# Two token blocks in another order at three stage boundaries of a hybrid decoder trunk

## The reference, cut to what matters

```
for l in range(2):
    h = rms_norm(x, attn_norm_g[l])
    x = x + hybrid_mixer(h, mem, w_in[l], ..., w_out[l])      # retention, forgetting attention, memory attention
    h = rms_norm(x, ffn_norm_g[l])
    if l % 2 == 0:
        x = x + (silu(h @ w_gate) * (h @ w_up)) @ w_down        # dense, D_FF = 2752
    else:
        x = x + moe_ffn(h, router_w, wg, wu, wd)                # top 2 of 8 experts
```

## Time and profile before

| what | value |
|---|---|
| median of three runs | 1327.45 us |
| fastest and slowest run | 1326.04 and 1327.48 us |
| span of the profiled execution | 1324.5 us |
| median less this span | 2.95 us |
| TensorE matmuls busy | 1248.4 us, 94% of the span |
| VectorE busy | 1011.2 us, 76% |
| ScalarE busy | 793.3 us, 60% |
| DMA, mean | 259 GB/s |
| mean granted clock of TensorE | 0.982 of full speed |

### The profile page before, as it was taken

How to read it: one execution, slowest core, us unless ns; L and a number is a source line. 1 busy time by engine, 2 the same in 40 slices (tenths; PEclk the granted TensorE clock), 3 DMA queues, 4 the chain that set the end, 5 groups by cost and what they waited for, 6 DMA issues and landing times.

```text
span 1324.5 us, 16360 instructions
## 1 busy us (share of the span) xinstructions
PE 1248.4 (94%) x6062; PEld 1037.6 (78%) x6062; DVE 1011.2 (76%) x988; ACT 793.3 (60%) x710; POOL 0.2 (0%) x4
## 2 busy tenths in 40 slices
PE   6998999999999869999999999989999998999996
PEld 4787788889787758887887887877887886887885
DVE  6878664444685778789788788887889886888885
ACT  4455354434446347677677677666667665667663
POOL 0000000000000000000000000000000000000000
PEclk9999899999999889999999999999999998999998
DMA  9842245546563138899899899898989998989970
GB/s 359 306 159 96 95 161 188 159 128 199 169 225 115 59 100 308 274 354 376 278 335 399 280 343 386 286 336 309 313 299 379 330 306 313 333 285 380 349 259 35
DMA packets 158798, 343.19 MB, mean 259 GB/s; under 512 B 5824, under 2 KB 47040, under 8 KB 158720
## 3 DMA queue, kind: packets, MB, share of 16 engines
q1 hardware_dynamic: 158720, 342.10, 74.3%
HBM read 341.02 MB, written 1.05 MB: 258 GB/s over the span
## 4 chain that ended last, share of the span: by engine, by line
PE 83%; DVE 10%; ACT 4%; issue 2%; DMA 0%; SPq 0%; DVEq 0%; ACTq 0%
PE ps L415 26%; PE ps L417 25%; PE ps L416 25%; DVE wlo L290 5%; ACT whi L283 3%; PE ps L644 1%; PE ps L465 1%; DVE scaled L1114 1%; PE ps L766 1%; PE ps L767 1%; PE ps L440 1%; PE ps L741 1%; PE ps L740 1%; DVE stlo L1124 1%; PE ps L514 0%
## 5 line engine op out<-in xcount | busy, mean ns | idle before, releaser
L290 DVE TENSOR_TENSOR wlo<-raw,whi 128x2048 fp32r<-128x2048 f32 (+3 forms) x356 | 741.3, 2100 | 237.6 <-ACT whi L283 237.2
L283 ACT ACTIVATE whi<-raw 128x2048 fp32r<-128x2048 f32 (+3 forms) x356 | 625.5, 1765 | 342.8 <-PE ps L417 341.3
L415 PE MATMUL ps<-whi,sthi 128*128 128x512 f32 (+4 forms) x1232 | 468.9, 381 | 21.7 <-DVE wlo L290 14.4
L417 PE MATMUL ps<-whi,stlo 128*128 128x512 f32 (+4 forms) x1232 | 457.9, 372 | 3.6 <-issue 3.6
L416 PE MATMUL ps<-wlo,sthi 128*128 128x512 f32 (+4 forms) x1232 | 458.5, 372 | 0.0
L415 PEld LDWEIGHTS ps<-whi,sthi 128*128 128x128 f32 x1232 | 233.8, 190 | 72.7 <-issue 22.7
L417 PEld LDWEIGHTS ps<-whi,stlo 128*128 128x128 f32 x1232 | 233.6, 190 | 39.0
L416 PEld LDWEIGHTS ps<-wlo,sthi 128*128 128x128 f32 x1232 | 234.3, 190 | 34.3
L415 PE MATMUL ps<-whi,hidhi 128*128 128x512 f32 (+1 forms) x440 | 176.6, 401 | 14.2 <-DVE wlo L290 11.4
L416 PE MATMUL ps<-wlo,hidhi 128*128 128x512 f32 (+1 forms) x440 | 172.3, 391 | 0.0
L417 PE MATMUL ps<-whi,hidlo 128*128 128x512 f32 (+1 forms) x440 | 172.2, 391 | 0.0
(11 more groups left out here) (191 smaller groups left out, 608.0 us busy)
## 6 DMA issues: line engine op xcount, KB each, us to landing
raw<-in_expert_w_down SPq DMA_DIRECT2D x80, 1024.0 KB, 6.8
raw<-in_expert_w_gate SPq DMA_DIRECT2D x64, 1024.0 KB, 7.3
raw<-in_expert_w_up SPq DMA_DIRECT2D x64, 1024.0 KB, 8.0
raw<-in_w_in SPq DMA_DIRECT2D x18, 1024.0 KB, 9.6
raw<-in_expert_w_gate SPq DMA_DIRECT2D x16, 768.0 KB, 6.1
raw<-in_expert_w_up SPq DMA_DIRECT2D x16, 768.0 KB, 5.1
raw<-in_dense_w_down SPq DMA_DIRECT2D x10, 1024.0 KB, 4.9
raw<-in_expert_w_gate SPq DMA_DIRECT2D x16, 640.0 KB, 4.2
```

The source lines that it names most:

```text
L283: eng.activation(whi[0:rows, n % SPLIT, 0:k * cols], raw[0:rows, n % RAW, 0:k * cols], ACT.Copy).then_inc(sem("hi_ready"), 1)
L290: eng.tensor_tensor(wlo[0:rows, n % SPLIT, 0:k * cols], raw[0:rows, n % RAW, 0:k * cols], whi[0:rows, n % SPLIT, 0:k * cols].bitcast(F32), ...
L415: pe.matmul(dst, xh, wh, start=start, stop=False)
L417: return pe.matmul(dst, xl, wh, start=False, stop=stop)
```

## The change

On TensorE, loads 2 and 3 of the out projection are taken as (2, block 0), (3, block 0), (2, block 1), (3, block 1). Between the last two stand the eight transposes of block 0's new `x`. The last two dense down loads go the same way. The units of a boundary are counted block by block: (0,0), (0,1), (1,0), (1,1). The first two loads of the dense gate and of the second input projection are taken block by block, and the eight transposes of block 1 stand behind the first twelve matmuls of block 0. Ahead of the router they stand right behind the out projection.

On ScalarE and VectorE, the split of the second load of the next stage moves into `next_turn`. VectorE has it behind block 0's units and ahead of the addition of block 1; ScalarE has it behind the squares of block 0 and ahead of block 0's units. ScalarE's squares of block 1 come ahead of block 1's units.

```diff
-                for q in range(4):
-                    m = n + 10 + q
-                    if q < 2:
-                        turn(f"out{l}", (2 * q, 2 * q + 1))
-                    pe.wait_ge(sem("lo_ready"), m + 1)
-                    for b in range(NB):
...
+                pe.wait_ge(sem("lo_ready"), n + 12 + 1)
+                mix_out(2, 0)
+                pe.wait_ge(sem("lo_ready"), n + 13 + 1)
+                mix_out(3, 0).then_inc(sem("block_summed"), 1)
+                mix_out(2, 1).then_inc(sem("weights_used"), 1)
+                turn(f"ffn{l}", (0, 1))
+                mix_out(3, 1).then_inc(sem("weights_used"), 1)
...
+            def first_gates(n):
+
+                for b in range(NB):
+                    for h in range(2):
+                        if b == 0:
+                            pe.wait_ge(sem("lo_ready"), n + h + 1)
+                        turned_in("ffn0", unit_of("ffn0", b, h))
+                        for k in range(4):
+                            last = product(ps[:, b, 0:CH[0]], P, stat(b, 4 * h + k), n + h, k, 4, CH[0], 0, CH[0],
+                                           start=(h == 0 and k == 0), stop=(h == 1 and k == 3))
+                        if b == NB - 1:
+                            last.then_inc(sem("weights_used"), 1)
+                        if b == 0 and h == 0:
+                            turn("ffn0", (2, 3))
...
+            pe.wait_ge(sem("lo_ready"), n + 1)
+            pe.wait_ge(sem("hid_lo"), NB * NCH - 1)
+            last_down(0, 0)
+            pe.wait_ge(sem("lo_ready"), n + 2)
+            last_down(1, 0).then_inc(sem("block_summed"), 1)
+            pe.wait_ge(sem("hid_lo"), NB * NCH)
+            last_down(0, 1).then_inc(sem("weights_used"), 1)
+            turn("att1", (0, 1))
+            last_down(1, 1).then_inc(sem("weights_used"), 1)
+
             mixer(1, IN1)
-            turn("ffn1")
+            turn("ffn1", (2, 3))
...
# ScalarE, next_turn
                 sum_squares(0)
-                used(act, n)
-                turn(name)
+                step(n - 1)
+                turn(name, (0, 1))
                 sum_squares(1).then_inc(sem("x_squared"), 1)
+                turn(name, (2, 3))
...
# VectorE, next_turn, inside the loop over the blocks
                     dve.tensor_tensor(xres[:, b, :], xres[:, b, :], flat(ps[:, at:at + 2, :]), ALU.add)\
                         .then_inc(sem("x_added"), 1)
-                turn(name)
-                if late is not None:
-                    step(late)
+                    turn(name, (2 * b, 2 * b + 1))
+                    if b == 0:
+                        step(n - 1)
...
# ScalarE and VectorE, ahead of next_turn
-                for q in range(3):
+                for q in range(2):
                     step(n + 10 + q)
```

More of the change, by code:

```diff
@@ L335, in build, with unit_of, place_of @@
         SCALED = {"att0": 0, "ffn0": 1, "att1": 2, "ffn1": 3}
-        UNITS = [(u % NB, u // NB) for u in range(2 * NB)]
+        def unit_of(name, b, half):
+            return 2 * b + half if name in X_ADDED else NB * half + b
+        def place_of(name, u):
+            return (u // 2, u % 2) if name in X_ADDED else (u % NB, u // NB)
         def turn_bank(name, u):
@@ L424, in turn @@
                 for u in units:
-                    b, half = UNITS[u]
+                    b, half = place_of(name, u)
                     src = xres if name in X_ADDED or name == "att0" else tok
@@ L621, in widths, with mix_out @@
-            def widths(kind, n, it, c, h, nb, par, bank, unit, fresh=None):
+                def mix_out(q, b):
+                    turned_in(f"out{l}", unit_of(f"out{l}", b, q // 2))
+                    for k in range(2):
+                        for half in range(2):
+                            last = product(ps[:, 2 * b + half, :], P, stat(b, 2 * q + k), n + 10 + q, k, 2, D,
+                                           half * W, (half + 1) * W, start=(q == 0 and k == 0), stop=(q == 3 and k == 1))
+                    return last
@@ new lines, in mixer @@
+                for q in range(2):
+                    turn(f"out{l}", (2 * q, 2 * q + 1))
+                    pe.wait_ge(sem("lo_ready"), n + 10 + q + 1)
+                    mix_out(q, 0)
+                    mix_out(q, 1).then_inc(sem("weights_used"), 1)
+                pe.wait_ge(sem("lo_ready"), n + 12 + 1)
[3 more added lines that the diff above has]
+                mix_out(2, 1).then_inc(sem("weights_used"), 1)
@@ L689, in _, with last_down @@
             n += 2
-            for h in range(2):
-                down(n + h, 0, NCH - 1, h, NB, NB * (NCH - 1), False, True)
-            turn("att1")
+            def last_down(h, b):
+                rows, nk, _ = ffn_shape("down", NCH - 1, h)
+                for k in range(nk):
+                    for half in range(2):
+                        last = product(ps[:, 4 + 2 * b + half, :], rows,
+                                       (hidhi[0:rows, b, 2 * h + k, :], hidlo[0:rows, b, 2 * h + k, :]), n + h, k, nk, D,
+                                       half * W, (half + 1) * W, start=False, stop=(h == 1 and k == nk - 1))
+                return last
+            pe.wait_ge(sem("lo_ready"), n + 1)
[7 more added lines that the diff above has]
+            last_down(1, 1).then_inc(sem("weights_used"), 1)
             mixer(1, IN1)
-            turn("ffn1")
+            turn("ffn1", (2, 3))
             pe.wait_ge(sem("router_lo"), 1)
@@ L1013, in _ @@
             n += 2
-            step(n)
             next_turn("att1", n + 1)
@@ L1209, in memory_turned, with next_turn @@
                 last.then_inc(sem("mk_T"), 1)
-            def next_turn(name, n, banks, late=None):
+            def next_turn(name, n, banks):
                 count = (n == DENSE0 - 1, n == IN1 - 1, n == MOE0 - 1).index(True)
```

31 lines of the change are left out of this document (19 added, 12 removed).

## The result

The changed kernel took 1330.78 us (median of seven runs, 1325.96 to 1332.5), the kernel before 1325.27 us beside it (seven runs, 1324.27 to 1327.48). The ratio is 1.0031, with a 95% interval of 1.0018 to 1.0045: 2.4 to 6.0 us slower. The span of its profiled execution is 1330.7 us against 1324.5.

The account below looks back on a forecast made before the run. TensorE, busy 94% of the span, was taken as the bound. Boundary shifts of -0.8, +0.5 and +3.95 us sum to +3.65 on 1327.45, giving 1331.1 us; own range 1329.6 to 1332.8, 8-in-10 range 1327.3 to 1332.8.

Parts of the forecast that it names:

- First boundary, -0.8: Out projection of layer 0 to dense gate: 0.8 us shorter, with bounds of -1.5 and 0.
- Second boundary, +0.5: Last two dense down loads to second input projection: 0.5 us longer by TensorE's waits, bounds -0.5 and +1.2.
- Third boundary, +1.45 by the waits: Out projection of layer 1 to router: 1.45 us longer by later units and logits, bounds +1.0 and +2.0.
- Third boundary, +2.5 by the clock: Router matmuls at 1.2 GHz after an emptier stretch: 2.5 us longer, at most 2.9, 0 if the clock stays.
- Rival 1: Third boundary: the clock holds through the emptier stretch, sum +1.15 us, 1328.6 us; chance 0.28.
- 472 to 474: Third boundary before the change: a row with twelve transposes and clock 1.00, set against a fall of the clock.
- Rival 2: Behind the router: clock still up when collecting matmuls start, 2.4 us off, sum -1.25, 1326.2 us; chance 0.10.
- The expert part passes the shift on: Expert part: TensorE busy for 795.63 of 820.70 us, so a shift at its start reaches the end.
- The row of waits for low parts: TensorE's waits for the low parts of the transposed units: 4.4 us at four places.
- the range's lower end of 1329.6: Lower end of the forecast's own range, 1329.6 to 1332.8 us, described as half of the 2.5 us clock term.

Follow-up runs that it names:

- e3: The changed kernel with VectorE's weight split behind block 1's addition instead of ahead of it, at all three boundaries; ratio 0.9987 to the kernel before.
- e2: The kernel before with the new order at the first and second boundaries only; ratio 0.9998 to the kernel before.
- e4: The changed kernel with eighteen extra matmuls, their sums never read, around block 1's transposes at the third boundary; ratio 0.9962 to the kernel before.
- e5: The kernel before with the new order at the third boundary only; ratio 1.0039 to the kernel before.
- e7: e3 with ScalarE rounding block 0's units ahead of its split at the second boundary and the third boundary's split moved out; ratio 0.9961 to the kernel before.
- e1: The kernel before with the new order at the first boundary only; ratio 0.9989 to the kernel before.
- e6: The kernel before with ten extra matmuls behind the logits' transposes and eight behind the ranking, sums never read; ratio 0.9956 to the kernel before.
- e9: e7 with e6's extra matmuls and VectorE's splits of the second and third expert loads behind the gathered rows; 1315.8 us against 1327.37 for the kernel before.
- e8: e7 with eighteen extra matmuls, sums never read, around block 1's transposes and behind logits and ranking; ratio 0.9929 to the kernel before.
- e10: The kernel before with six extra matmuls behind the ranking, sums never read; ratio 1.0027 to the kernel before.

## Why the prediction was right

The sum was +3.65 us with a time of 1331.1; the three boundaries measured +4.08 and the kernel 1330.78. The sum and its mechanism stand. That the two times agree within 0.3 us is in part luck: the forecast starts from 1327.45, the median of the first three runs, while the seven have 1325.27, and the medians differ by 5.5 us and not 3.65. By its steps:

- **First boundary, -0.8.** Measured -1.09. The mechanism is as written: ScalarE's and VectorE's queues hold the weight split between block 0's units and block 1's addition, and TensorE idled 0.8 us instead of the 1.0 that I had. e3 shows the cause: with the split behind the addition, these 0.8 us went.
- **Second boundary, +0.5.** By the waits it is +0.55 (e2, e4), with 0.94 and 0.83 us idle where I had 1.2 and 1.0. The changed kernel's own trace had +1.06, since the clock fell behind the 0.94 us wait. I had looked for a fall of the clock at the third boundary only; the term was short by 0.5 us in this trace, inside its bounds, and right in e2 and e4.
- **Third boundary, +1.45 by the waits.** Measured 1.22, from e4.
- **Third boundary, +2.5 by the clock.** Measured 2.9 (4.11 less 1.22). The clock fell at 471.4, ahead of the transposes and not just ahead of the router, so they were slow too. Rival 1, that it holds, fell: in the changed kernel and in e5 the router ran at 1.2 GHz. In e7, with 1.31 us idle ahead of block 1's transposes instead of 3.62, the clock held through the router. The sentence of the Trainium skill ("TensorE: Matmul & The Clock Gate", "What's actually happening") that activity releases the throttle agrees with e4, where eighteen matmuls in the idle time kept the clock at 2.4 GHz and no other edit was made. Against it the prediction set 472 to 474, where the clock held over a shorter gap with twice as many transposes. Three traces with more idle time there (the changed kernel, e5, e3) had the fall and e7 with less idle time had not; but e1 had a fall with the old gap, so the clock at this boundary isn't settled by the order alone.
- **Rival 2, activity carried over to the collecting matmuls.** It could not be seen here, as the clock fell at the router. Its price of 2.4 us was wrong in this kernel: e6 made those matmuls fast and the boundary stayed at 37.8 us, since a split on VectorE stood in the same chain. With that out of the way too, the stretch of e9 is 2.2 us shorter than that of e7, where the filling alone (e8) had won nothing.
- **The expert part passes the shift on.** It did, but not unchanged. In the profiled pair it was 4.27 us longer: 1.6 of it the clock at its first matmuls, and 2.5 the two loop turns (108.84 and 109.84 us against 108.33 and 107.83). The 2.5 us are the clock too. TensorE's idle time in the two turns is the same, 13.3 us, but behind each turn it worked at 1.2 GHz for some 5 us before and some 7.8 in the changed kernel, and half of the difference, for two turns, is 2.8 us. Stretches of 12 us of TensorE show it by their granted clock, the number behind the busy time: 0.72 in the two of before and 0.57 in the two of the changed kernel.

```profile
893.00:905.00 12.00, 10.25 (x38) 0.72 0.68 254
1101.00:1113.00 12.00, 10.15 (x36) 0.72 0.68 269
894.00:906.00 12.00, 8.88 (x23) 0.57 0.87 346
1105.00:1117.00 12.00, 9.38 (x25) 0.57 0.71 282
```

The order doesn't bring this about as such: e3 and e7 have it too, and their turns take 106.49 and 109.69, and 107.05 and 106.82 us. So I don't count the 2.5 as an effect of the change. Of the changed kernel's seven executions the fastest (1325.96 us) had a mean granted clock of 0.982 and the four slowest 0.975 to 0.978. The range was no narrower for the kernel before, once it had run more often: 1323.61 to 1330.05 us in the 25 executions beside e1.

Two readings of the prediction were off and changed nothing in its sum. The row of waits for low parts, 4.4 us at four, was taken for the boundaries, but two of its four waits (1.47 us at 136.0 and 1.66 at 445.0) lie elsewhere, and the router's 2.01 and 0.66 stand in another row. And the range's lower end of 1329.6 doesn't come out of its terms: with half of the 2.5 off, the sum gives 1329.85.

What the prediction got from reading the queues, not the waits, was the sign: TensorE had 6.0 us of idle time at the three boundaries, which looks like something to win, and the new order moves the wait from block 0's addition to block 1's.

## What to carry to other kernels

When work is reordered so that a producer finishes one part early, read the in-order queues of the engines behind it from the early part to the late one: whatever stands between them, here a 2.3 us weight split, is added to the late part. At the first boundary, where matmuls stand between, the new order still won 1.1 us; at the third, where none do, it lost 4.1. Move such an instruction to where its own consumer is still far away (e7), before judging the order itself. And count an idle stretch of TensorE for more than its length, since the matmuls behind it may run at half clock: at the third boundary the waits cost 1.2 us and the clock 2.9.

## What the runs showed of the hardware that I had not expected

- **A wait that belongs to a place in TensorE's program.** Seven kernels have no extra matmuls (before, changed, e1, e2, e3, e5, e7). Their loop's turns take 106.5 to 109.8 us, and at both turns of all seven a second wait of 0.7 to 2.9 us stands behind the eighth matmul of the turn. In the four with eighteen extra matmuls ahead of the loop (e4, e6, e8, e9) it is gone from both turns, which take 103.8 to 106.6 us. With six extra matmuls it is six matmuls earlier and 3.5 and 3.8 us long. What it is, no view of the profile names, and I leave it open. What is shown is that matmuls whose sums nobody reads, in idle time, made the kernel 0.44% faster (e6) or 0.27% slower (e10). An experiment that adds or removes instructions ahead of a loop should be judged by its stretches as well as by its time.
- **The clock fell behind much less idle time than at the third boundary.** At the second boundary of the changed kernel the only idle time in the eleven microseconds ahead of the fall was 0.94 us, behind eight transposes and six matmuls of 64 rows, and the clock was at 1.2 GHz for 3.4 us; in e2 and e4, with the same order, it stayed at 2.4 GHz. So it is a matter of the execution as well as of the kernel.
- **It fell at 495.3 too, within the first expert matmul of the changed kernel**, after a stretch at 2.4 GHz from 492 in which TensorE was half idle. In e9 it did not fall there, though TensorE waited 1.24 us behind its first expert matmuls.
